# Products of the identity with a matrix of ones, put into TensorE's waits at fifteen places of a transformer block

## What is computed

```
mod = silu(c) @ w_ada + b_ada                      # six rows of 1024
h   = modulate(rms_norm(x, norm1_g), shift1, scale1)
p   = h @ w_in
y   = concat(rwkv7_mix(p[:, :RWKV_COLS]), fox_mix(p[:, RWKV_COLS:])) @ w_out
x   = x + gate1 * y
h   = modulate(rms_norm(x, norm2_g), shift2, scale2)
logits = h @ w_router + b_router
top_val, top_idx = top_k(logits, 4);  gates = softmax(top_val)
# each token goes to its 4 experts e:
gu  = xblk @ w_gate_up[e] + b_gate_up[e]
act = min(gate, 7) * sigmoid(1.702 * gate) * (clip(up, -7, 7) + 1)
y_e = act @ w_down[e] + b_down[e]
x   = x + gate2 * (sum over experts of gates * y_e)
out = rms_norm(x, final_g)
```

## Time and profile before

| what | value |
|---|---|
| median of 3 runs | 1403.41 us (1400.06 to 1404.39) |
| the profiled execution's own time | 1401.43 us |
| its span, first to last instruction | 1399.7 us |
| TensorE busy with matmuls | 1156.9 us, 83% |
| TensorE busy with weight loads | 557.4 us, 40% |
| VectorE (DVE), ScalarE (ACT), GpSimd (POOL) | 282.8, 218.2, 76.6 us |
| granted TensorE clock, mean | 0.878 of full speed |
| moved by DMA | 457.78 MB, mean 327 GB/s |

### The profile page before, as it was taken

How to read it: one execution, slowest core, us unless ns; L and a number is a source line. 1 busy time by engine, 2 the same in 40 slices (tenths; PEclk the granted TensorE clock), 3 DMA queues, 4 the chain that set the end, 5 groups by cost and what they waited for, 6 DMA issues and landing times.

```text
span 1399.7 us, 28975 instructions
## 1 busy us (share of the span) xinstructions
PE 1156.9 (83%) x11263; PEld 557.4 (40%) x11264; DVE 282.8 (20%) x817; ACT 218.2 (16%) x485; POOL 76.6 (5%) x192
## 2 busy tenths in 40 slices
PE   4989998898689667776799999986668889869993
PEld 1868885653434212211244444431112334323441
DVE  0255432123521100100021111210001112101212
ACT  2321122121112000100021212110001111101211
POOL 8000000010000000000000000000000000000000
PEclk9999999668789977878899999998778889979997
DMA  9432129525859999999979998999999997999175
GB/s 354 173 121 92 61 93 330 184 91 194 330 215 423 422 422 421 422 422 422 422 308 423 422 402 334 421 422 422 422 422 423 422 422 316 408 423 421 71 320 246
DMA packets 81120, 457.78 MB, mean 327 GB/s; under 512 B 6903, under 2 KB 8017, under 8 KB 31905
## 3 DMA queue, kind: packets, MB, share of 16 engines
q1 hardware_dynamic: 79280, 452.00, 79.4%
q0 software_dynamic: 1296, 4.74, 0.9%
q10 hardware_dynamic: 512, 0.60, 0.1%
HBM read 455.19 MB, written 2.11 MB: 327 GB/s over the span
## 4 chain that ended last, share of the span: by engine, by line
PE 54%; DMA 24%; SPq 13%; DVE 4%; issue 2%; ACT 2%; ACTq 1%; DVEq 0%
DMA raw<-in_w_down 18%; PE bank L1734 16%; PE bank L1747 9%; SPq L349 8%; PE bank L1319 7%; SPq L353 5%; PE bank L1776 3%; PE bank L1648 2%; PE bank L1707 2%; DMA raw<-in_w_gate_up 2%; DMA odd<-in_w_gate_up 2%; PE bank L1284 2%; PE bank L1756 2%; DMA raw<-in_final_g 1%; PE bank L1469 1%
## 5 line engine op out<-in xcount | busy, mean ns | idle before, releaser
L1747 PE MATMUL bank<-raw,aT 128*32 128x256 f32 x3328 | 236.1, 431 | 79.0 <-DMA raw<-in_w_down 76.4
L1734 PE MATMUL bank<-raw,xT 128*32 128x512 f32 x1600 | 213.1, 660 | 52.9 <-DMA raw<-in_w_gate_up 37.7
L1734 PE MATMUL bank<-odd,xT 128*32 128x512 f32 x1664 | 208.5, 630 | 32.4 <-DMA odd<-in_w_gate_up 32.3
L1747 PEld LDWEIGHTS bank<-raw,aT 128*32 128x32 f32 x3328 | 112.6, 120 | 214.0 <-DMA raw<-in_w_down 127.8
L1222 DVE TENSOR_TENSOR gated<-bank,bias_i 128x256 f32<-128x256 f32 x51 | 21.6, 424 | 749.2 <-PE bank L1756 749.2
L1734 PEld LDWEIGHTS bank<-raw,xT 128*32 128x32 f32 x1600 | 48.8, 114 | 180.8 <-DMA raw<-in_w_gate_up 91.5
L1319 PE MATMUL bank<-hT,raw 128*128 128x256 f32 (+1 forms) x496 | 114.7, 390 | 1.9 <-ACT hT L565 1.9
L1734 PEld LDWEIGHTS bank<-odd,xT 128*32 128x32 f32 x1664 | 48.5, 112 | 154.7 <-DMA odd<-in_w_gate_up 74.0
L1319 PEld LDWEIGHTS bank<-hT,raw 128*128 128x128 f32 (+1 forms) x496 | 93.9, 192 | 20.1 <-issue 5.3
L512 POOL TENSOR_TENSOR gatehot<-onehot,gates 128x128 f32<-128x128 f32 x102 | 38.6, 399 | 958.1 <-PE bank L1723 926.1
L758 ACT ACTIVATE evy<-bank 128x256 f32<-128x256 f32 x52 | 20.0, 384 | 448.4 <-PE bank L1747 448.4
(11 more groups left out here) (376 smaller groups left out, 902.4 us busy)
## 6 DMA issues: line engine op xcount, KB each, us to landing
raw<-in_w_gate_up SPq DMA_DIRECT2D x128, 1024.0 KB, 22.1
raw<-in_w_down SPq DMA_DIRECT2D x128, 1024.0 KB, 18.3
odd<-in_w_gate_up SPq DMA_DIRECT2D x128, 1024.0 KB, 25.8
raw<-in_w_ada SPq DMA_DIRECT2D x12, 2048.0 KB, 9.3
raw<-in_w_in SPq DMA_DIRECT2D x7, 2048.0 KB, 8.1
raw<-in_w_out SPq DMA_DIRECT2D x2, 2048.0 KB, 10.8
raw<-in_w_in SPq DMA_DIRECT2D x1, 1056.0 KB, 5.3
x_sb<-in_x SPq DMA_DIRECT2D x1, 1024.0 KB, 4.9
```

The lines of the kernel that those rows point to most:

```text
L1734: g = mm(bank[0][j * CAP:(j + 1) * CAP, :], xT[:, u % 2, u // 2, :], gu_slab(u, p)[:, j * NC:(j + 1) * NC], start=u == 0, stop=u == KT - 1)
L1747: g = mm(bank[1][j * CAP:(j + 1) * CAP, 0:NQ], aT[:, k % 4, k // 4, :], dn_slab(u)[:, at:at + NQ], start=k == 0, stop=k == KT - 1)
```

## The change

A new function `keep_warm(b, count)` issues `count` products of the identity (stationary, 128x128) with the matrix of ones, read four times over (moving, 128x512), each into the whole of bank b. Nothing reads the result, and the products signal no semaphore. 48 such products are added to TensorE's list, and nothing else is moved or removed. In `turn_probs` for heads 3 to 7 a wait is added ahead of them, for DVE's copy of that head's own scores (`s_ev`), since the products overwrite their bank.

```
+            def keep_warm(b, count):
+                for _ in range(count):
+                    mm(bank[b][:, :], ident[:, :], ones[:, :].unsqueeze(1).to_broadcast([P, CT, P]),
+                       start=True, stop=True)
...
             def turn_probs(h):
+                if h >= 3:
+                    pe.wait_ge(S("s_ev"), h + 1)
+                    keep_warm(h % 2, 2)
                 pe.wait_ge(S("pr_ready"), h + 1)
...
             for n in range(3):
+                keep_warm(1, 2)
                 apply_rest(n)
...
             turn_probs(4)
+            keep_warm(0, 2)
             pe.wait_ge(S("tx_ev"), 1)
...
             i.then_inc(S("z_mm"), 1)
+            keep_warm(0, 2)
             pe.wait_ge(S("tx_ev"), 3)
...
             i.then_inc(S("y_mm"), 1)
+            keep_warm(1, 2)
             for u in range(NH, NU):
                 outputs(u, False)
...
             i.then_inc(S("bias_T"), 1)
+            keep_warm(1, 10)
             pe.wait_ge(S("h2_ready"), TT)
...
             i.then_inc(S("router_mm"), 1)
+            keep_warm(1, 10)
             pe.wait_ge(S("sel_ready"), 1)
...
             i.then_inc(S("gT_mm"), 1)
+            keep_warm(1, 2)
             pe.wait_ge(S("gT_ready"), 1)
...
             (the four products with b_down, line 1695)
+            keep_warm(1, 4)
```

## The result

The changed kernel takes 1410.62 us in the median of 5 runs (1406.36 to 1414.23), the kernel before 1403.41 us (1400.06 to 1405.28). The ratio is 1.0051 with a 95% interval of 1.0033 to 1.0069: slower by half a per cent. The forecast was 1399.8 us and "same"; the time lies outside the stated range.

A forecast was written before the change was run, and what follows sets the result against it. TensorE, often at half clock, was taken to bound the stages before the experts. Mixer -2.8 and router -1.0 us gave 1397.6; one clock fall, +2.2, made 1399.8 us, likeliest "same", range 1395.0 to 1406.5.

The forecast's parts named there:

- What bounds it; one to one to the end: Before the experts TensorE's unwaiting time is on the path; every microsecond changed before 394.95 us passes whole to the end.
- What a product costs: A pair of added products takes 1.74 us at full clock or 3.62 at low; ten take 8.7 or 18.1.
- Mixer, -2.8: Up to the centering products, the full clock's gains less the pairs' costs come to -2.8 us.
- First ten, +2.3: Before h2's transposes: ten products take 8.7 us and end at 366.6, h2 being ready at 364.26; +2.3 us.
- the transposes behind it, -1.4: h2's sixteen transposes at full clock: 4.36 us up to line 1675 become 2.9, limited by ACT's copies; -1.4 us.
- Line 1675 at the full clock, -1.2: The router's logits, 4.44 us before, were taken as 3.2 us at full clock; -1.2 us.
- Ranks to first gate-and-up, -1.1 and -3.4: Ranks halve, -1.1 us; gather, transposes and first gate-and-up start at full clock, -1.1, -0.3 and -2.0, net -3.4.
- The deduction for falls, +2.2: One clock fall, at the second ten products (between logits and ranks), was counted: 4.5 us at half speed, +2.2 us.
- two tens too many: Rival: the router's tens, 8.7 us each, exceed their waits and clock falls leave them unpaid; 1407.6 us; 15 in 100 for slower.
- Its point of decision: That rival decides once a product's mean in the second ten, between logits and ranks, is above 1.1 us.
- My three signs of being wrong: Clock 0.50 in the mixer's last heads, a ten over 11 us, or end moving over 2 us against first down products.
- The rule on transposes: Skill page: transposes don't count as activity, so h2's transposes and line 1675 would be slow; 1402.4 us, 5 in 100.

The follow-up runs named there:

- waits_early: waits_cover with pairs of products also in the softmax waits of heads 0 to 2; 1383.49 us, ratio 0.9867 to the kernel before.
- mixer_only: The changed kernel without its four calls around the router, leaving the mixer's 22 products; 1403.22 us, ratio 0.9993 to the kernel before.
- no_tens: The changed kernel without the two calls of ten products around the router; 1406.12 us, ratio 1.0016 to the kernel before.
- singles: tens_fit with every pair of products in the mixer made a single product; 1407.37 us, ratio 1.0025 to the kernel before.
- waits_only: tens_fit with mixer pairs only in the softmax waits of heads 3, 5 and 6; 1394.40 us, ratio 0.9940 to the kernel before.
- waits_cover: waits_only plus four products before mix_out and one before the first item, the last four cut to two; 1395.67 us, ratio 0.9925 to the kernel before.
- head3_only: waits_only with head 3's pair as the only one in the mixer; 1395.69 us, ratio 0.9954 to the kernel before.
- tens_fit: The changed kernel with its two tens around the router cut to six and four products; 1401.70 us, ratio 0.9988 to the kernel before.

## Why the prediction was wrong

- **What bounds it; one to one to the end: right, within the spread.** From the first down to the end all eighteen kernels need 999.0 to 1002.5 us. What is lost before the experts shows in the total, give or take these 3.5 us; 1.1 of them fell to the change.
- **What a product costs: right at the lower clock, a little low at the full one.** Forecast 1.74 us a pair, measured 1.91 in most places (1.72 at one); the ten 8.85 for 8.7.
- **Mixer, -2.8: wrong, +1.2 in the profile** (scores(4) to the centering products 54.1 us for 52.9). Of this miss of 4.0 us, 3.2 lie between head 3's and head 4's transposes, where the sum had -3.8 and the profile has -0.6. Some 1.5 us of the 4.0 are the dearer pairs, and 1.5 the fall at 281.4, which made head 4's pair 3.36 us and for which this part of the sum had nothing. Of the rest apply_rest has some, whose thirds took 1.07 and not 0.9 us. What I did not ask is whether the pairs were needed: the inverse's use to the outputs takes 30.3 us at the low clock without pairs, 31.5 at a mean clock of 0.95 with them, and 18.5 (waits_early) at the full clock without.
- **First ten, +2.3, and the transposes behind it, -1.4: right** (+2.3 and -1.6).
- **Line 1675 at the full clock, -1.2: wrong, +1.1.** The clock fell at 369.9, earlier than the "fall at the second ten" that I had priced at 2.2 us. Logits and second ten together: 11.9 + 2.2 = 14.1 us by my sum, 15.6 measured, 9.4 before.
- **Ranks to first gate-and-up, -1.1 and -3.4: wrong.** Ranks to gather gave -0.4, since the last four outlasted DVE's list after one more fall (390.7 us). Gather to item gave -0.8. The first gate-and-up gave -0.2 and not -2.0: the clock had fallen yet again.
- **The deduction for falls, +2.2: the step that failed most.** It was four falls where I had taken off one. Two of them, at the logits and ahead of the first gate-and-up, stood where I had named a doubt; the one at 281.4 came behind the inverse's use, and the one at 390.7 in the last four, where I had none. By the terms above they cost about 8 us (1.5, then 2.4 in the logits and 1.5 in the second ten, 0.7, and 1.8), not 2.2. The sum of the profile's stages is +7.3 us against -1.6; of the difference of 8.9 the falls make 5.7, the pairs and pieces of the mixer 2.5 and the experts 1.1, and mix_out gives 0.5 back. The rival "two tens too many" had the mechanism and the sign at 1407.6 us, and I gave it 15 in 100. Its point of decision, a mean of over 1.1 us a product in the second ten, was not even reached (1.04): the loss did not need it. My three signs of being wrong did not come either (a low clock in the mixer's last heads, a ten of over 11 us, an end moved by over 2 us against the first down; it was 10.4 us, and 1.1): they looked for one large miss, and it was several small ones.
- **The rule on transposes** (the Trainium skill, "TensorE: Matmul & The Clock Gate", section "Part 4: PE-mode transpose"): the clock stayed at 1.00 through the sixteen transposes of h2, which does not decide it, since the ten stood right before them. What the row of before showed, a rise with transposes alone on TensorE, stands, and the profiles without a first ten repeat it: in mixer_only the mean clock is 0.50 in the 2 us ahead of these transposes, 0.53 in their first 3.4 us and 1.00 from their end on, and no_tens has the same. This case does not agree with the page there.

## What to carry to other kernels

Fill TensorE's waits with products only up to the length of the wait, measured at the full clock, and begin with the first wait behind which the clock falls, not with the work that is slow afterwards: six pairs in softmax waits gave 1.2% together, while eight pairs between pieces of work cost 12 us, as much as the higher clock could give there. Too few in a wait can be worse than none: in the profile of singles the clock fell all the same and the later products cost double. Where the clock is a matter of chance, compare stage lengths over several profiles and include the stages ahead of the change, look at the spread of the totals for two groups, and count each doubtful stretch as a fall before the sum is trusted.

## What the runs showed of the hardware

- The granted clock can stay at 0.50 for 27 us in which PE is busy without a break (waits_only, 270.50 to 297.80), and the same instructions run at 1.00 throughout in another profile (waits_early, 257.75 to 283.81). In both the clock was at 1.00 when the inverse's use began (waits_only, 260.15 to 267.77). So being busy did not raise it there for 27 us, and having it is worth keeping. What differs from run to run to let it fall there is not shown.
- Part of the run-to-run spread is this: in waits_cover and head3_only the quickest executions are those with the highest mean clock (0.909 and 0.910 against 0.886 to 0.896; 0.903 against 0.887 to 0.897). waits_early spread over 1380.9 to 1384.1 us in four runs. The kernel before spread over 1399.5 to 1410.2 in its many runs; where its spread comes from is not shown.
- The logits, 32 passes with a weight load of 128 columns for 32 columns of product, had the clock fall during them or at their end in the kernel before (371.7 us), in the change (369.9) and in tens_fit (mean 0.53 from 371.5 to 375.0), in the last two with ten or six products of 512 columns a few us ahead of them.
